# The joint of mix stage and up-projection: the last tile's norm moved up, weight parts behind it, identity transposes between the products

## The reference

```python
mix = jnp.concatenate([attn, conv], axis=-1) @ w_o[l]
h = layer_norm(ALPHA * h + mix, ln1_g[l], ln1_b[l])
ffn = conv_gated_mlp(h, w_up[l], ffn_conv_w[l], ffn_conv_b[l], w_down[l])
# conv_gated_mlp
z = causal_depthwise_conv(h @ w_up, conv_w, conv_b)
g, val = jnp.split(z, 2, axis=-1)
return (jax.nn.gelu(g, approximate=False) * val) @ w_down
```

## Time and profile before

| What | Value |
|---|---|
| median of three runs | 1905.46 us |
| the profiled execution's own time | 1907.91 us |
| its span, first to last instruction | 1906.1 us |
| mean granted TensorE clock | 0.991 |
| PE busy (matmul) | 1866.2 us, 98% |
| DVE busy | 1534.6 us, 81% |
| ACT busy | 950.7 us, 50% |
| POOL busy | 906.7 us, 48% |
| u_mm matmuls (L2356) | 3696 in 1245.2 us of busy time |

### The profile page before, as it was taken

How to read it: one execution, slowest core, us unless ns; L and a number is a source line. 1 busy time by engine, 2 the same in 40 slices (tenths; PEclk the granted TensorE clock), 3 DMA queues, 4 the chain that set the end, 5 groups by cost and what they waited for, 6 DMA issues and landing times.

```text
span 1906.1 us, 26980 instructions
## 1 busy us (share of the span) xinstructions
PE 1866.2 (98%) x8632; PEld 1531.4 (80%) x8632; DVE 1534.6 (81%) x1939; ACT 950.7 (50%) x1482; POOL 906.7 (48%) x666
## 2 busy tenths in 40 slices
PE   8999999999999899999999899999999999999998
PEld 7788888777777688888888688888888788888886
DVE  8877994699998888888988987888888755676787
ACT  3455662777778544444445444444444432232453
POOL 2159994266675355444545544444443765520000
PEclk9999999999999899999999999999999999999999
DMA  7411123634563423333334332322234654587554
GB/s 271 180 44 44 44 83 121 207 118 145 174 206 121 141 108 126 133 110 110 118 141 168 112 113 99 116 93 105 99 116 140 199 159 138 170 261 244 186 170 144
DMA packets 201828, 265.80 MB, mean 139 GB/s; under 512 B 12320, under 2 KB 131360, under 8 KB 200480
## 3 DMA queue, kind: packets, MB, share of 16 engines
q1 hardware_dynamic: 188096, 229.32, 36.4%
q10 hardware_dynamic: 13664, 35.66, 5.0%
HBM read 177.18 MB, written 87.75 MB: 139 GB/s over the span
## 4 chain that ended last, share of the span: by engine, by line
PE 58%; issue 17%; DVE 10%; POOL 7%; ACT 4%; DMA 2%; SPq 1%; POOLq 0%; DVEq 0%; ACTq 0%
PE d_y L2785 20%; PE u_mm L2356 20%; PE a_mm L250 15%; POOL u_w_sum L1338 2%; POOL u_w_sum L1336 1%; PE m_y L2405 1%; ACT m_ce L1730 1%; POOL u_s L1356 1%; POOL u_s L1359 1%; ACT m_tps L1722 1%; DVE m_stat L2140 1%; POOL u_s L1353 1%; DVE m_top L2184 1%; DVE m_den L2197 1%; DVE u_w_lo L1900 1%
## 5 line engine op out<-in xcount | busy, mean ns | idle before, releaser
L2356 PE MATMUL u_mm<-u_forms,u_w_hi 128*128 128x512 f32 x2464 | 763.9, 391 | 11.5 <-issue 4.6
L2356 PEld LDWEIGHTS u_mm<-u_forms,u_w_hi 128*128 128x128 f32 x2464 | 463.9, 189 | 112.9 <-issue 11.8
L2356 PE MATMUL u_mm<-u_forms,u_w_lo 128*128 128x512 f32 x1232 | 481.3, 391 | 0.0
L2785 PE MATMUL d_y<-d_wd,d_a_hi 128*128 128x512 f32 x1232 | 379.6, 389 | 1.5 <-DVE d_a_lo L1033 1.5
L250 PE MATMUL a_mm<-a_hT,a_w_hi 128*128 128x512 f32 x896 | 278.2, 392 | 2.1 <-DVE a_hT L535 2.1
L2356 PEld LDWEIGHTS u_mm<-u_forms,u_w_lo 128*128 128x128 f32 x1232 | 232.4, 189 | 48.8
L2785 PEld LDWEIGHTS d_y<-d_wd,d_a_hi 128*128 128x128 f32 x1232 | 231.1, 188 | 50.1 <-DVE d_a_lo L1033 1.9
L2785 PE MATMUL d_y<-d_wd,d_a_lo 128*128 128x512 f32 x616 | 239.6, 389 | 0.0
L1940 DVE SCALAR_TENSOR_TENSOR u_y<-u_z,u_taps,u_y 128x1024 f32<-128x1024 f32 x176 | 222.6, 1287 | 10.4 <-DVE u_z L1954 3.2
L1336 POOL TENSOR_TENSOR u_w_sum<-u_w_raw 128x512 f32<-128x512 f32 x44 | 58.8, 1337 | 295.7 <-DMA u_w_raw<-w_up 295.7
L250 PEld LDWEIGHTS a_mm<-a_hT,a_w_hi 128*128 128x128 f32 x896 | 166.7, 188 | 37.7 <-DVE a_hT L535 3.7
(11 more groups left out here) (244 smaller groups left out, 2954.6 us busy)
## 6 DMA issues: line engine op xcount, KB each, us to landing
u_w_raw<-w_up SPq DMA_DIRECT2D x44, 1024.0 KB, 4.8
d_a_raw<-gated_scr SPq DMA_DIRECT2D x56, 704.0 KB, 5.2
gated_scr<-u_s SPq DMA_DIRECT2D x88, 256.0 KB, 2.0
d_wd_raw<-w_down SPq DMA_DIRECT2D x88, 256.0 KB, 5.2
gated_scr<-u_gy SPq DMA_DIRECT2D x44, 256.0 KB, 2.1
a_xs<-x SPq DMA_DIRECT2D x16, 512.0 KB, 5.1
m_h_in<-h_scr SPq DMA_DIRECT2D x16, 512.0 KB, 4.0
h_scr<-m_r SPq DMA_DIRECT2D x16, 512.0 KB, 4.7
```

The lines of the kernel that those rows point to most:

```text
L2356: last = nc.tensor.matmul(mm[BANK[s]][:], w[:, s, k, :], forms[:, POS[s], part, k, :], start=(s in FRESH and k == 0 and w is w_hi and part ...
L2785: m = nc.tensor.matmul(dy[u % BANKS][:], a[:, u % 2, k, :], wd[:, ph % 2, k, part, :], start=(k == 0 and a is a_hi and part == HI_PART), s ...
```

## The change

On DVE `tail_norm(d)` moves up to stand directly behind `tail_norm(c)`, and `make_c22` moves behind the low part of Q4. On ACT `out_T(d)` moves up behind `out_T(c)`, and `take_c11` goes behind both remaining `right_hi`. On SP the refill of the weights moves behind the stores of c's turned rows and d's rows. On PE `turn_rows(d)` moves ahead of Q2, and a new function `keep_turning` transposes the identity matrix into the PSUM tile `m_y`, which nobody reads any more: 24 times, 8 times and 36 times.

```diff
@@ sync
             store_turned(b)
             store_row(c)
-            refill(Step(0, 0, 0), 1)
             store_turned(c)
             store_row(d)
+            refill(Step(0, 0, 0), 1)
             store_turned(d)
@@ scalar
             out_T(c)
+            out_T(d)
             act.wait_ge(resid_ok, NT)
             right_hi(0, Q4)
-            take_c11(opening)
-            out_T(d)
             act.wait_ge(h1_st[1], 16 * (NT // 2 + 1))
             act.wait_ge(h1_st[0], 16 * (NT // 2 + 1))
             right_hi(0, Q3)
+            take_c11(opening)
@@ vector
             tail_norm(c)
+            tail_norm(d)
             weights_lo(opening, Q2)
             right_lo(0, Q2)
             dve.wait_ge(rlo_ok, FORMS[0].index(Q2) + 1)
             nc.vector.tensor_tensor(spare, spare, stage[:, 2, :, :], ALU.subtract).then_inc(t4_ok, 1)
             weights_lo(opening, Q4)
             weights_lo(opening, Q3)
-            tail_norm(d)
             make_u2(opening)
             make_u3(opening)
-            make_c22(opening)
             dve.wait_ge(h1_ok, NT)
             right_lo(0, Q4)
+            make_c22(opening)
@@ tensor
+            def keep_turning(times):
+
+                pe.wait_ge(resid_ok, NT)
+                for k in range(times):
+                    nc.tensor.transpose(ym[:, (k % KT) * P:(k % KT + 1) * P], ident[:], ident[:])
@@ tensor
             turn_rows(c)
+            keep_turning(24)
+            turn_rows(d)
+            keep_turning(8)
             product(opening, Q2, 0)
-            turn_rows(d)
+            keep_turning(36)
             product(opening, Q4, 0)
             product(opening, Q3, 0)
```

## The result

The changed kernel took 1909.32 us (median of 15 runs, 1908.16 to 1913.43), the kernel before in the same comparison 1906.98 (15 runs, 1903.62 to 1914.72). The ratio is 1.0019, with a 95% interval of 1.0012 to 1.0026: slower by 3.6 us, between 2.3 and 5.0. The forecast was 1906.3 with a range of 1902.3 to 1909.6, a loss of 0.8 us that could not have been told from none. The time lies just inside the range, and the loss is real: 2.3 to 5.0 us where the sum had 0.8.

What follows compares the result with a forecast made beforehand. TensorE, 98% busy, was taken as the bound, so Q3's start and clock decide: -0.9 us (Q3 sooner) + 1.7 (clock) = +0.8, giving 1908.7 profiled and, 2.45 lower for the median, 1906.3 us; range 1902.3 to 1909.6.

Steps and rivals of the forecast that it cites:

- rival 2: At Q3: POOL's sums hold up DVE's low pass (+0.9), clock price doubles to 3.4; +2.7 us, 1908.2; chance 0.11.
- DVE's sum and d's norm 6.3 us sooner: On DVE before Q2: the order changes, the total stays; d's norm ends at about 627.9 instead of 634.27.
- The identity transposes hold the clock: On PE up to Q4: full clock kept, so Q4 takes 2.7 us, not 5.46; the 36 take 4.3 us.
- Rival 3: On PE before Q3: transposes don't hold the clock and become work in the path; +5 us, 1910.5; chance 0.10.
- At full clock their price is nothing: On PE before Q4: the 68 identity transposes fit inside waits, the 36 with only 0.2 us of cover.
- Q4 0.6 us sooner: On PE: Q4 starts at 638.1 instead of 638.74, as c22 now stands behind its low part.
- SP, the refill and the store behind it: On SP: refill issued at 634.3, store of d's turned rows at 634.73, landing after 6.4 us at 641.1.
- Then 2.35 us of DVE: DVE's low pass for Q3 after the store lands; Q3 starts at 643.7, 0.9 us sooner (bounds 641.4 and 644.7).
- I charge 1.7: On PE at Q3: a 2.9 us idle piece lowers the clock, costing 1.7 us (bounds 0 and 3.4).
- The sum of the joint: Around Q3: -0.9 us for its sooner start, +1.7 for the clock, 0 for all else: +0.8 us.
- Next step's weights covered: The refill lands 3.3 us later, yet PE takes the next Q1's low part without waiting; price nothing.
- rival 1: Before Q3: the store lands early, about 639 to 640, without clock loss; -2.1 to -3.2 us, 1902.8; chance 0.17.

Runs made afterwards that it cites:

- e2: The changed kernel without the 68 identity transposes, d's rows still turned ahead of Q2; 1909.42 us, ratio to the kernel before 1.0012.
- e3: The changed kernel with 36 more identity transposes between Q4 and Q3; 1907.17 us, ratio to the kernel before 0.9999.
- e4: The changed kernel with POOL's sums of the next step held until Q3's low right part is made; 1911.31 us, ratio to the kernel before 1.0018.
- e5: The kernel before, unchanged, timed against itself and profiled a second time; 1907.40 us, ratio 1.0000.
- e1: The changed kernel with SP's store of d's turned rows ahead of the refill of the weights; 1907.64 us, ratio to the kernel before 1.0003.
- e8: The kernel before with 12, 16 and 16 identity transposes behind c's transposes, Q2 and d's transposes, orders unchanged; 1910.57 us, ratio to the kernel before 1.0015.
- e10: The kernel of e8, timed and profiled once more; 1911.50 us, ratio to the kernel before 1.0021.
- e6: The changed kernel with low weight parts ahead of d's norm, refill ahead of the stores, 36 instead of 24 first transposes; 1906.21 us, ratio to before 0.9989.
- e11: The kernel of e6, timed and profiled once more; 1905.12 us, ratio to the kernel before 0.9979.
- e7: The kernel of e6 without any identity transposes; 1905.95 us, ratio to the kernel before 0.9992.
- e9: The changed kernel, unchanged, timed and profiled a second time; 1911.04 us, ratio to the kernel before 1.0018.

## Why the prediction was wrong

The path was the one forecast: Q3's start set by DVE's low part behind the late store, then a low clock over Q3. Two terms of the sum were too small, DVE's pass beside POOL and the clock at Q3; together they are rival 2, to which I had given 0.11.

- DVE's sum and d's norm 6.3 us sooner: right. d's transposes start 3.8 us behind c's norm (forecast 4.0).
- The identity transposes hold the clock and delay nothing themselves: right (1.00 from 624 to 640; the 36 took 3.93 us, forecast 4.3). Rival 3 is out. But the 2.5 us by which they shortened Q4 went into the wait before Q3, and e2 has the joint 2.2 us shorter without them: "At full clock their price is nothing" is true of Q4's start and not of the whole. The Trainium skill (TensorE: Matmul & The Clock Gate, Part 4: PE-mode transpose) says that full rate doesn't engage for transposes. The traces of this case disagree, for float32 transposes: in the earlier trace rows the granted clock rose from 0.50 to 1.00 while TensorE did nothing else, and in e3 36 of them kept it at 1.00.
- Q4 0.6 us sooner: 0.8.
- SP, the refill and the store behind it: right. The refill was issued 9.61 us behind c's norm, forecast 9.64; the store landed 6.7 us after its issue, forecast 6.4.
- "Then 2.35 us of DVE": this step failed. It was 3.27, since the late refill puts POOL's sums beside this very pass; e4 gives it back as 2.29. The prediction had named this hold-up, with up to 1.3 us, and put it at nothing in the sum, because in the earlier trace rows it was POOL that took longer; there DVE's pass had begun first (636.36 against 637.14), here a sum of POOL had (639.95 against 640.09). Q3 was to start 0.9 us sooner and started 0.2 later, just outside the bounds given: 0.9 for the pass and 0.3 for the landing, less 0.1.
- "I charge 1.7" for the clock at Q3: mis-sized. The first twelve matmuls from 643.46 took 5.1 us, where before they took 2.8, so 2.3. The wait was 3.9 us, not 2.9. By the prediction's own measure the three stretches from 640 to 652 (0.70, 0.50 and 0.94) give 3.4, rival 2's figure, of which 1.1 was hidden in the wait. The 1.7 had been read from one execution: in the second profile of the kernel before (e5) the clock is 1.00 from 624 to 628 and Q2 starts at full rate, behind the same pieces of waiting. e3 measures the term alone at 2.3 us in the trace, and takes the ratio from 1.0019 to 0.9999.
- The sum of the joint: forecast +0.8, measured +2.5 in the trace (44.59 against 42.06), +3.6 (2.3 to 5.0) in the times.
- The base: I set the change on a median of three runs, 1905.46. With fifteen it is 1906.98. Half of the 3.0 us between 1906.3 and 1909.32 is this.
- Next step's weights covered: right for the changed kernel, but only since Q3 was late. As soon as Q3 is early (e1) this cover is gone and 1.74 us appear. The prediction gave it a price of nothing on the ground of a late Q3, and carried that into rival 1, where Q3 is early.

What stays open: for e1, e2, e8 and e10 the times lie 2 to 3 us above what their one profiled joint would give, against intervals of 1.7 to 2.1 us to either side. The clock's draw, seen in e8 against e10, can make a part of it; that it makes all was not shown. Another part may lie in the down-projection, where PE's wait for weight pieces is 2.6, 0.6, 1.6 and 1.1 us in these four profiles, and absent in e6 and e11. Against that, e3 and e7 have 1.7 us of it each and no such excess. The profiled executions can't settle it, for up to c's norm, where all kernels are alike, they take between 620.7 and 626.4 us.

## What to carry to other kernels

When a norm or a store is moved up, look at every queue that it shares: here the work was early, and its last store stood behind a transfer whose gate the same move had delayed by 3.2 us. Only with both early, the store and the gate of the refill, did the times show a gain (e6 and e11: 0.1 to 0.2%); with the store alone (e1) they showed none, though its joint was shorter. Filling waits of TensorE with idle transposes gained something here directly ahead of the product on the path (e3: 0.2% against the changed kernel). Put earlier, they took the low clock from where it was hidden and lengthened the wait in which it fell next (e2 against the changed kernel), and in the kernel before they cost 0.15 to 0.2% (e8, e10). And a price read from one execution's clock is weak: two executions of one kernel differed in where it fell.

## What the runs showed of the hardware

- Float32 transposes of 128x128 alone kept the granted clock at 1.00: 36 of them between Q4 and Q3, 0.109 us each (e3), against a fall to 0.50 without.
- A wait of about 3 us before Q3 let the clock fall in one execution (e10, 3.01) and not in two others (e8, 2.96; e4, 2.94); waits of 3.9 and 4.1 us (changed, e9) let it fall both times. The wait of about 2 us before d's transposes did so in e10 (the eight in 1.97 us) and not in e8 (1.09 us).
- A 128x2048 DVE subtraction took 3.27 us beside POOL's tensor_tensor and 2.29 without it (e4); the POOL sum that began inside the pass took 3.33 us, against 1.29 for the same sum in e4. In the earlier trace rows and in the changed kernel the sum that began inside the pass ended 1.1 us after it, and the pass was long only where a sum had begun first (639.95 against 640.09). It looks as if the one that comes second waits; why, no run shows.
